# Second attention: GpSimd instead of VectorE makes the low halves of 16 weight tiles

## The chip, the cores and the metric

The kernel runs on one core of a Trainium2 chip. The time is device microseconds (us) of one execution; runs are compared by their median. The engines go by the names of the profile: PE (TensorE, matrix products and transposes), DVE (VectorE), ACT (ScalarE), POOL (GpSimd) and SP (issues most DMAs). PEld is PE's loading of stationary tiles, which runs beside its products.

## The reference, cut to what matters

Two transformer blocks run one after the other on 1024 tokens of width 1024. The change lies in the second. Its attention part is:

```
h = rms_norm_2(x, norm1)
qa, ka, va, fa, qc, kc, vc, gates = split(h @ w_in)
o_a = forgetting_attention(qa, ka, va, log_sigmoid(fa + bias))  # 8 heads, causal
o_b = chunk_band_attention(qc, kc, vc, rel_bias)                # 8 heads, band of 640 keys
g_a, g_b = split(sigmoid(gates))
x = x + (g_a * (o_a @ w_branch_a) + g_b * (o_b @ w_branch_b)) @ w_out
```

All products of weights are float32. The kernel splits a weight tile w and the activations x into a rounded high half and a low half, low = value - high, and adds three products: high by high, high by low and low by high.

## The kernel before, in words

A *unit* is one 128-column tile of a weight matrix, 8 blocks of 128 rows, against all 1024 tokens: 48 matmuls of 128x512. For unit n the tile passes through four hands. SP loads it into `wraw[n % 2]` (`load_w`, L334). ACT copies it rounded into `wh[n % 2]` (`split_hi`, L341), once unit n - 2, which used the buffer before, has been multiplied. Then someone makes `wl[n % 2] = wraw - wh` and raises the semaphore `w_lo`. In all the rest of the program that is POOL (`split_lo`, L346). Last, PE multiplies, and DVE takes the sum out of PSUM.

The second attention (`a2_program_pe`, `_act`, `_dve`, `_sp`; 1826 to 2267 us) runs 8 *pairs* of heads, 4 of the causal kind and then 4 of the band kind, each in 8 steps n of 128 queries. In a step PE makes the scores of step n+2 (L1982, L1985), transposes the probabilities of step n four key blocks at a time (`turn`, L2005; each waits for DVE's scaling and for a free PSUM bank 4), and after each second step multiplies with the values (L2024). Between these PE does `fill`: 1 to 8 matmuls (L1954) of the 16 gate units `U_GATES` to `U_GATES + 15`, so that it has work while the others make the softmax. `FILL` says how many; the units come to an end at 16 fixed places (`UNIT_ENDS`) in the pairs 0 to 6.

DVE does in step n, in this written order: `reciprocal` of the row sums (L2200), two scalings of `pbuf` by them (L2204, `tensor_scalar`, SBUF to SBUF, 128 to 1024 columns wide), the two maxima of step n+2 (L2148, reads PSUM and `bias2`), the low halves of the gate weight tiles whose unit ended a step before (`gate_lo`, L2186), in steps 0 and 5 the low half of an attention output (`low`, L2179), and the copies of the turned probabilities of one head (L2132, PSUM to `pt2`). Where a unit has ended, `gate_evac` (L2168) takes its sum out. That is at the step's end at most places; the next thing on DVE is then the next step's L2200 and L2204, or, at a change of pairs, `begin` and its maxima.

ACT does the copies of the other head (L2134), the exponentials (L2076), and `split_hi` at the end of a step in which a unit ended. `gate_evac(u)` on DVE and `split_hi(u + 2)` on ACT wait for the same event, the last matmul of unit u.

The tile that `gate_lo(u)` or `split_lo` makes there is that of unit u + 2, for u = 0 to 15; the last two are the first tiles of `w_branch`. PE asks for it one whole unit later. SP's load of unit u + 3 waits for `w_lo` of the tile that lay in the same buffer.

Of the kernel before, what the change touches and what calls it, by code (L numbers as in the profile page):

```python
# [8 lines left out]
F32 = mybir.dt.float32  # L9
F32R = mybir.dt.float32r  # L10
ALU = mybir.AluOpType
# [56 lines left out]
U_BRANCH = U_QKV2 + 40  # L68
U_OUT2 = U_BRANCH + KT
U_UP2 = U_OUT2 + KT  # L70
# [39 lines left out]
def build_program(nc, a, out):  # L110
    ctx = ExitStack()
    with ctx:
# [3 lines left out]
        def at(name, offset_kb, shape, dt=F32):  # L116
            return nc.alloc_sbuf_tensor_at(name, shape, dt, offset=base + int(offset_kb * KB))

        def sem(name):
            return ctx.enter_context(nc.semaphore(name))  # L120
# [7 lines left out]
        wh = at("wh", 64, [P, 2, KT, P], F32R)  # L128
        wl = at("wl", 72, [P, 2, KT, P], F32R)
        wraw = at("wraw", 80, [P, 2, KT, P])  # L130
# [56 lines left out]
        def bank2(slot):  # L187
            return ps[:, 2 * slot:2 * slot + 2, :]
# [118 lines left out]
        w_hi = sem("w_hi")  # L307
        w_lo = sem("w_lo")
# [34 lines left out]
        def split_lo(pool, n, s, first=False):  # L343

            pool.wait_ge(w_hi, n + 1)
            nc.gpsimd.tensor_tensor(wl[:, s, :, :], wraw[:, s, :, :], wh[:, s, :, :].bitcast(F32),  # L346
                                    ALU.subtract).then_inc(w_lo, 1)
# [100 lines left out]
        def apart(eng):  # L448


            eng.sem_inc(marks, 1)
# [1344 lines left out]
        def keys_of(b, n):  # L1796
            return range(0 if b < FOX_PAIRS else max(0, n - 4), n + 1)

        def groups_of(b, n):
            return range((len(keys_of(b, n)) + 3) // 4)  # L1800

        def bias_part(b, n):
            size = P * len(keys_of(b, n))
            first = P * (4 - n) if b >= FOX_PAIRS and n < 4 else 0
            return slice(first, first + size)
# [11 lines left out]
        def unit_ends():  # L1817

            ends, made = {}, sum(LEAD)
            for b in range(PAIRS):  # L1820
                made += TURN_FILL[b] + BEGIN[b]
                for n in range(TT):
                    groups = 2 * len(groups_of(b, n))
                    for k in range(groups):
                        count = FILL[b][n][k]
                        for u in range(made // UNIT, (made + count) // UNIT):
                            ends.setdefault((b, n, 2 * k // groups), []).append(u)
                        made += count
            assert made == 16 * UNIT, made
            return ends  # L1830

        UNIT_ENDS = unit_ends()
# [69 lines left out]
        U_GATES = U_QKV2 + QKV2  # L1902
# [218 lines left out]
        def turned_copy(eng, steps, b, n, m, g):  # L2121

            count = min(4, len(keys_of(b, n)) - 4 * g)
            first = keys_of(b, n)[0] + 4 * g
            a2_pe.wait(eng, f"t{b}{n}{m}{g}", 0)
            old = TT // 2 * b + n // 2 - 2
            if old >= 0:
                a2_pe.wait(eng, f"o{old // 4}{old % 4}", 0)
            to = pt2[:, n // 2 % 2, first:first + count, m, n % 2 * P:n % 2 * P + P]
            of = ps[:, TURN_BANK[b, n, m, g], 0:count * P].rearrange("p (k q) -> p k q", k=count)  # L2130
            if m:
                ins = nc.vector.tensor_copy(to, of)  # L2132
            else:
                ins = nc.scalar.activation(to, of, ACT.Copy)  # L2134
            steps.done(ins, f"pt{b}{n}{m}{g}")

        def a2_program_dve(dve):

            def maxima(b, n):
                size = P * len(keys_of(b, n))  # L2140
                a2_pe.wait(dve, f"s{b}{n}", 0)
                step = TT * b + n
                if step >= 3:
                    ob, on = divmod(step - 3, TT)
                    a2_pe.wait(dve, f"t{ob}{on}1{groups_of(ob, on)[-1]}", 0)
                for m in range(2):
                    apart(dve)
                    a2_dve.done(nc.vector.tensor_tensor_reduce(  # L2148
                        pbuf[:, step % 3, m, 0:size], ps[:, 2 * m:2 * m + 2, :].rearrange("p a n -> p (a n)")[:, 0:size],
                        bias2[:, m, bias_part(b, n)], -1.0, 3e38, ALU.add, ALU.min, negmax2[:, n, m:m + 1]),  # L2150
                        f"mx{b}{n}{m}")

            def begin(b):

                dve.wait_ge(a2_bias, 32 * (b + 1) + 96 * max(0, b + 1 - FOX_PAIRS))
                if b >= FOX_PAIRS:
                    for m in range(2):
                        a2_dve.done(nc.vector.memset(bias2[0:64, m, 576:640], NEG), f"e{b}{2 * m}")
                        a2_dve.done(nc.vector.memset(bias2[64:128, m, 0:64], NEG), f"e{b}{2 * m + 1}")
                    a2_dve.wait(dve, f"e{b}3", 0)  # L2160
                maxima(b, 0)

            def gate_evac(u):

                n = U_GATES + u
                dve.wait_ge(mm_done, n + 1)
                dve.wait_ge(stage_stored[0], STAGES1 + 16 * (4 + u))
                nc.vector.tensor_tensor(stage[:, 0, :], bank2(3), rstd[:, :], ALU.mult).then_inc(evac_done, 1)  # L2168

            def low(b, h):  # L2170

                a2_act.wait(dve, f"ot{b}{h}", 0)
                if b < PAIRS - 1:
                    dve.wait_ge(parked_stored[h], 32 * b)
                    lo, hi = ost_lo[:, h, :], ost[:, h, :]
                else:
                    part = slice(h * HALF, (h + 1) * HALF)
                    lo, hi = xl[:, b, part], xh[:, b, part]
                a2_dve.done(nc.vector.tensor_tensor(lo, ps[:, 5, :], hi.bitcast(F32), ALU.subtract), f"xl{b}{h}")  # L2179

            def gate_lo(u):

                n = U_GATES + u + 2
                dve.wait_ge(w_hi, n + 1)
                dve.wait_ge(w_lo, n)
                nc.vector.tensor_tensor(wl[:, n % 2, :, :], wraw[:, n % 2, :, :], wh[:, n % 2, :, :].bitcast(F32),  # L2186
                                        ALU.subtract).then_inc(w_lo, 1)

            for s in range(2):
                dve.wait_ge(hi_stored[s], 16 * 8)  # L2190
                dve.wait_ge(lo_stored[s], 16 * 8)
                dve.wait_ge(stage_stored[s], STAGES1 + 16 * 4)
            lows = []
            begin(0)
            for b in range(PAIRS):
                maxima(b, 1)
                for n in range(TT):
                    size = P * len(keys_of(b, n))
                    a2_act.wait(dve, f"ex{b}{n}1", 0)
                    a2_dve.done(nc.vector.reciprocal(rowsum2[:, n, :], rowsum2[:, n, :]), f"rl{b}{n}")  # L2200
                    a2_dve.wait(dve, f"rl{b}{n}", 0)
                    for m in range(2):
                        part = pbuf[:, (TT * b + n) % 3, m, 0:size]
                        a2_dve.done(nc.vector.tensor_scalar(part, part, rowsum2[:, n, m:m + 1], None, ALU.mult),  # L2204
                                    f"sc{b}{n}{m}")
                    if n + 2 < TT:
                        maxima(b, n + 2)
                    for u in UNIT_ENDS.get((b, n, 0), ()):
                        gate_evac(u)
                    for u in lows:  # L2210
                        gate_lo(u)
                    lows = []
                    if n == 0 and b:
                        low(b - 1, 1)
                    if n == 5:
                        low(b, 0)
                    for g in groups_of(b, n):
                        turned_copy(dve, a2_dve, b, n, 1, g)
                    for u in UNIT_ENDS.get((b, n, 1), ()):
                        gate_evac(u)  # L2220
                    lows += [u for part in range(2) for u in UNIT_ENDS.get((b, n, part), ())]
                    if n == TT - 1 and b + 1 < PAIRS:
                        begin(b + 1)
            low(PAIRS - 1, 1)
# [542 lines left out]
        def _(pool):  # L2767
# [92 lines left out]
            for u in range(QKV2):  # L2860
                split_lo(pool, U_QKV2 + 2 + u, (U_QKV2 + u) % 2)
                if of_qk(u):
                    c = qk_index(u)
                    pool.wait_ge(hl_hi, c + 1)
                    if c >= 2:
                        pool.wait_ge(lo_stored[u % 2], 16 * (c // 2))
                    nc.gpsimd.tensor_tensor(ls[:, u % 2, :], stage[:, u % 2, :], hs[:, u % 2, :].bitcast(F32),
                                            ALU.subtract).then_inc(hl_lo, 1)
            for n in range(U_BRANCH + 2, U_UP2 + 2):
                split_lo(pool, n, n % 2)  # L2870
            with pool.Fori(0, DOWN2 - 1) as c:
                for k in range(2, 4):
# [425 lines left out]
```

## Time and profile before

| | before |
|---|---|
| median of 3 runs | 3165.24 us (3164.25 to 3165.67) |
| the profiled execution: time, span | 3167.0 us, 3165.3 us |
| PE busy | 3027.9 us, 96% of the span |
| DVE busy | 1525.4 us, 48% |
| ACT busy | 968.9 us, 31% |
| POOL busy | 634.3 us, 20%, 276 instructions |
| in 1825 to 2260 us: PE, DVE, ACT, POOL busy | 405.9, 241.1, 175.1, 2.4 us |

Busy time is time in which the engine worked on an instruction; what counts for the kernel's time is which engine the others wait for at a given place. The stretch in the last row is the second attention: PE has work for 406 of its 435 us, and POOL has one instruction in it, the last low half made before the attention began.

### The profile page before, as it was taken

The numbers are of one execution on the slowest core, as the hardware profiler recorded it, in microseconds if no ns is written. First come the engines' busy times: TensorE is split into PE (matmuls) and PEld (weight loads), VectorE is DVE, ScalarE is ACT, GpSimd is POOL, SyncE is SP. The second block draws the span as 40 slices with busy tenths as digits, with TensorE's granted clock in tenths as the row PEclk, the third lists the DMA queues.
The fourth block names the chain that finished last, engine by engine and source line by source line (L and its number), as shares of the span: only waits on it lengthen the run. The fifth ranks groups of instructions, "written<-read, shape, count | busy, mean of one in ns | idle before, by whom it ended". The sixth has DMA issues, their size and how long they took to land.

```text
span 3165.3 us, 48821 instructions
## 1 busy us (share of the span) xinstructions
PE 3027.9 (96%) x20514; PEld 2431.4 (77%) x20514; DVE 1525.4 (48%) x1859; ACT 968.9 (31%) x1438; POOL 634.3 (20%) x276
## 2 busy tenths in 40 slices
PE   8999988888999999999899999999899999999999
PEld 6877867777788888888678867666688888888887
DVE  3166677722644444445711145555553444444445
ACT  3155555623422222222411143334332211111112
POOL 4311122312321222122143300000022222122211
PEclk9999999999999999999899999999999999999999
DMA  6533410022411111111454533444544310111111
GB/s 206 164 99 108 146 70 25 25 76 62 151 47 40 60 46 46 46 40 40 128 168 129 170 113 116 129 143 128 199 138 137 116 49 31 53 53 53 46 33 67
DMA packets 235008, 292.80 MB, mean 93 GB/s; under 512 B 10057, under 2 KB 182226, under 8 KB 234842
## 3 DMA queue, kind: packets, MB, share of 16 engines
q1 hardware_dynamic: 219866, 243.22, 25.1%
q10 hardware_dynamic: 14976, 47.19, 3.9%
q8 instruction: 126, 2.06, 0.3%
q14 instruction: 40, 0.33, 0.0%
HBM read 209.86 MB, written 80.51 MB: 92 GB/s over the span
## 4 chain that ended last, share of the span: by engine, by line
PE 84%; DVE 6%; issue 5%; ACT 2%; DMA 2%; POOL 1%; SPq 0%; DVEq 0%; ACTq 0%; POOLq 0%
PE ps L369 62%; PE ps L1954 4%; PE ps L541 4%; PE ps L1385 4%; PE ps L2005 2%; PE ps L2024 2%; PE ps L1982 1%; PE ps L1448 1%; PE ps L1985 1%; DMA wraw<-in_w_in 1%; DMA residual<-src 1%; DVE cb L2567 1%; DVE y L2463 1%; DVE stage L2168 0%; PE ps L1426 0%
## 5 line engine op out<-in xcount | busy, mean ns | idle before, releaser
L346 POOL TENSOR_TENSOR wl<-wraw,wh 128x1024 fp32r<-128x1024 f32 x151 | 369.1, 2445 | 1672.0 <-ACT wh L341 1672.0
L369 PE MATMUL ps<-xh,wh 128*128 128x512 f32 x2192 | 683.5, 393 | 12.1 <-POOL wl L346 5.2
L369 PE MATMUL ps<-xl,wh 128*128 128x512 f32 x2192 | 678.1, 391 | 0.0
L369 PE MATMUL ps<-xh,wl 128*128 128x512 f32 x2192 | 677.7, 390 | 0.0
L369 PEld LDWEIGHTS ps<-xh,wh 128*128 128x128 f32 x2192 | 410.1, 189 | 110.9 <-issue 12.0
L369 PEld LDWEIGHTS ps<-xl,wh 128*128 128x128 f32 x2192 | 413.4, 189 | 86.8
L369 PEld LDWEIGHTS ps<-xh,wl 128*128 128x128 f32 x2192 | 413.1, 188 | 86.9
L341 ACT ACTIVATE wh<-wraw 128x1024 fp32r<-128x1024 f32 x167 | 177.0, 1060 | 928.2 <-PE ps L369 860.5
L2463 DVE TENSOR_TENSOR y<-ps,y 128x1024 f32<-128x1024 f32 x208 | 253.3, 1222 | 240.3 <-PE ps L369 240.1
L2366 POOL TENSOR_TENSOR dl<-draw,dh 128x2048 fp32r<-128x2048 f32 x25 | 119.1, 4765 | 521.2 <-ACT dh L2362 521.2
L2508 DVE SCALAR_TENSOR_TENSOR cb<-ub,cols,cb 128x1024 f32<-128x1024 f32 x88 | 130.6, 1484 | 61.1 <-ACT cb L2545 56.0
L369 PE MATMUL ps<-dh,fh 128*128 128x512 f32 x480 | 149.4, 392 | 6.0 <-DVE y L2463 6.0
L369 PE MATMUL ps<-dl,fh 128*128 128x512 f32 x480 | 148.0, 389 | 0.0
L369 PE MATMUL ps<-dh,fl 128*128 128x512 f32 x480 | 147.9, 389 | 0.0
L2498 DVE TENSOR_TENSOR ub<-ps,rstd 128x1024 f32<-128x1024 f32 x44 | 53.9, 1225 | 171.9 <-PE ps L369 171.7
L2567 DVE TENSOR_TENSOR cb<-ps,rstd 128x1024 f32<-128x1024 f32 x32 | 39.2, 1225 | 198.0 <-PE ps L369 194.1
L2148 DVE CUSTOM_DVE_ANT_0 pbuf<-ps,bias 128x640 f32<-128x640 f32 (+7 forms) x128 | 85.5, 705 | 97.5 <-PE ps L1990 49.6
L2362 ACT ACTIVATE dh<-draw 128x2048 fp32r<-128x2048 f32 x25 | 47.8, 1913 | 235.3 <-PE ps L369 235.3
L2005 PE MATMUL ps<-ident,pbuf 128*128 128x128 f32 x528 | 93.8, 286 | 20.2 <-DVE pbuf L2204 9.6
L369 PEld LDWEIGHTS ps<-dh,fh 128*128 128x128 f32 x480 | 89.0, 188 | 29.4 <-DVE y L2463 11.5
L2005 PEld LDWEIGHTS ps<-ident,pbuf 128*128 128x128 f32 x528 | 60.9, 143 | 59.3 <-DVE pbuf L2204 17.1
L369 PEld LDWEIGHTS ps<-dl,fh 128*128 128x128 f32 x480 | 90.1, 188 | 19.0
(345 smaller groups left out, 4402.2 us busy)
## 6 DMA issues: line engine op xcount, KB each, us to landing
wraw<-in_w_up SPq DMA_DIRECT2D x76, 512.0 KB, 3.9
wraw<-in_w_in SPq DMA_DIRECT2D x67, 512.0 KB, 4.2
draw<-in_w_down SPq DMA_DIRECT2D x27, 1024.0 KB, 5.0
residual<-src ACTq DMA_DIRECT2D x32, 512.0 KB, 5.0
proj<-stage SPq DMA_DIRECT2D x30, 512.0 KB, 3.0
qk_hi<-hs ACTq DMA_DIRECT2D x24, 512.0 KB, 2.8
qk_lo<-ls SPq DMA_DIRECT2D x24, 512.0 KB, 2.9
kh<-qk_hi SPq DMA_DIRECT2D x48, 256.0 KB, 6.9
```

What stands on the lines that cost most here:

```text
L341: nc.scalar.activation(wh[:, s, :, :], wraw[:, s, :, :], ACT.Copy).then_inc(w_hi, 1)
L346: nc.gpsimd.tensor_tensor(wl[:, s, :, :], wraw[:, s, :, :], wh[:, s, :, :].bitcast(F32), ALU.subtract).then_inc(w_lo, 1)
L369: mm = nc.tensor.matmul(ps[:, bank + h, :], w, x[:, h * HALF:(h + 1) * HALF], start=start and k == 0, stop=stop and k == 2)
L541: return nc.tensor.matmul(to, left, right, **kw)
L1385: ins = mm(ps[:, 2 * fill_slot(u) + h, :], w[:, s, kt, :], x[:, kt, h * HALF:(h + 1) * HALF], start=kt == 0 and part == 0, stop=kt == KT - ...
L1954: ins = mm(ps[:, 6 + h, :], w[:, s, kt, :], x[:, kt, h * HALF:(h + 1) * HALF], start=kt == 0 and part == 0, stop=kt == KT - 1 and part == 2)
L2005: ins = nc.tensor.transpose(ps[:, bank, (k - 4 * g) * P:(k - 4 * g + 1) * P], pbuf[:, (TT * b + n) % 3, m, k * P:(k + 1) * P], ident[:, :])
L2148: a2_dve.done(nc.vector.tensor_tensor_reduce(pbuf[:, step % 3, m, 0:size], ps[:, 2 * m:2 * m + 2, :].rearrange("p a n -> p (a n)")[:, 0:size],
L2366: nc.gpsimd.tensor_tensor(dl[:, :, :], draw[:, :, :], dh[:, :, :].bitcast(F32), ALU.subtract)\
L2463: nc.vector.tensor_tensor(y[:, m, :], bank2(2 + m % 2), y[:, m, :], ALU.add).then_inc(down_added, 1)
L2508: ff1_dve.done(nc.vector.scalar_tensor_tensor(out=cb[:, r, :], in0=ub[:, r, 2 - back:T + 2 - back], scalar=col_at("conv_w", (2 - back) * 2 ...
L2567: nc.vector.tensor_tensor(cb[:, 0, :], bank2((U_UP2 + t) % 2), rstd[:, :], ALU.mult)\
```

## The change

DVE no longer makes any low half. POOL's program gets the 16 calls instead, all in one loop with those that followed. Instructions of PE, ACT and SP, their order and what they wait for stay as they are.

```diff
 # a2_program_dve, gone:
-            def gate_lo(u):
-
-                n = U_GATES + u + 2
-                dve.wait_ge(w_hi, n + 1)
-                dve.wait_ge(w_lo, n)
-                nc.vector.tensor_tensor(wl[:, n % 2, :, :], wraw[:, n % 2, :, :], wh[:, n % 2, :, :].bitcast(F32),
-                                        ALU.subtract).then_inc(w_lo, 1)
...
                         maxima(b, n + 2)
                     for u in UNIT_ENDS.get((b, n, 0), ()):
                         gate_evac(u)
-                    for u in lows:
-                        gate_lo(u)
-                    lows = []
...
-                    lows += [u for part in range(2) for u in UNIT_ENDS.get((b, n, part), ())]
...
 # the program of GpSimd:
-            for n in range(U_BRANCH + 2, U_UP2 + 2):
+            for n in range(U_GATES + 2, U_UP2 + 2):
                 split_lo(pool, n, n % 2)
```

On DVE, at the end of the first gate unit (the unit's sum `stage` is taken out, then the next step's reciprocal, scalings and maxima, then the low half). The lines of the two versions differ by 9; `x2` marks two alike.

```order
 L2132 COPY pt_181<-ps 128x128
 L2168 TENSOR_TENSOR stage<-ps,rstd 128x1024
-L2200 RECIPROCAL rowsum_187<-rowsum_187 128x2
-L2204 TENSOR_SCALAR pbuf<-pbuf,rowsum_187 128x768 x2
+L2191 RECIPROCAL rowsum_187<-rowsum_187 128x2
+L2195 TENSOR_SCALAR pbuf<-pbuf,rowsum_187 128x768 x2
 L2148 ISA pbuf,negmax_186<-ps,bias_182 128x1024
 L2148 ISA negmax_186 128x1
 L2148 ISA pbuf,negmax_186<-ps,bias_182 128x1024
 L2148 ISA negmax_186 128x1
-L2186 TENSOR_TENSOR wl<-wraw,wh 128x1024
 L2179 TENSOR_TENSOR ost_lo<-ps,ost 128x512
```

One row goes, L2186; what stood behind it, `low` (L2179) and the copies, follows the maxima at once. There are 16 such places.

On POOL, around the end of the projections of the second block. Before:

```order
L346 TENSOR_TENSOR wl<-wraw,wh 128x1024 [waits w_hi]
L2867 TENSOR_TENSOR ls<-stage,hs 128x1024 [waits lo_stored1,hl_hi]
L346 TENSOR_TENSOR wl<-wraw,wh 128x1024 [waits w_hi] x20
L2871 UNCONDITIONAL_BRANCH
L2871 ISA
```

And now:

```order
L346 TENSOR_TENSOR wl<-wraw,wh 128x1024 [waits w_hi]
L2854 TENSOR_TENSOR ls<-stage,hs 128x1024 [waits lo_stored1,hl_hi]
L346 TENSOR_TENSOR wl<-wraw,wh 128x1024 [waits w_hi] x36
L2858 UNCONDITIONAL_BRANCH
L2858 ISA
```

The row of 20 low halves (the last 2 projection tiles, the first 2 gate tiles and 16 of later stages) has become one of 36: each of the new 16 waits for `w_hi`, that is for ACT's copy of its own tile, and for nothing else.

## Rows read from the trace of the kernel before

**Rows 1.** The page: the chain that ended last, by engine.

```profile
PE 84%; DVE 6%; issue 5%; ACT 2%; DMA 2%; POOL 1%; SPq 0%; DVEq 0%; ACTq 0%; POOLq 0%
```

**Rows 2.** Groups of the second attention (1825 to 2260 us): busy, mean ns, idle.

```profile
L2186 DVE TENSOR_TENSOR wl<-wraw,wh 128x1024 fp32r<-128x1024 f32 x16 | 19.5, 1221 | 0.0
```

**Rows 3.** Instructions on tile `wl`: ns min/median/max.

```profile
L346 POOL TENSOR_TENSOR wl<-wraw,wh x151: 2342/2402/3369, 14.3 to 3093.8; 128x1024 fp32r<-128x1024 f32 x151
```

**Rows 4.** Timeline of unit end 1857: start, us, engine, line [idle before].

```profile
1857.20 1.06 ACT L341 ACTIVATE wh<-wraw 128x1024 fp32r<-128x1024 f32 x1 [1.20 <-PE ps L1954]
...
1858.47 1.15 DVE L2204 TENSOR_SCALAR pbuf<-pbuf,rowsum 128x768 f32<-128x768 f32 x2
...
1859.14 0.66 PE L2005 MATMUL ps<-ident,pbuf 128*128 128x128 f32 x4
...
1861.82 1.22 DVE L2186 TENSOR_TENSOR wl<-wraw,wh 128x1024 fp32r<-128x1024 f32 x1
...
1864.39 0.41 PE L2005 MATMUL ps<-ident,pbuf 128*128 128x128 f32 x2 [1.10 <-DVE pt L2132]
```

**Rows 5.** Timeline of unit end 2101, a band pair.

```profile
2101.65 1.06 ACT L341 ACTIVATE wh<-wraw 128x1024 fp32r<-128x1024 f32 x1 [0.89 <-PE ps L1954]
...
2102.92 1.02 DVE L2204 TENSOR_SCALAR pbuf<-pbuf,rowsum 128x640 f32<-128x640 f32 x2
...
2103.53 0.66 PE L2005 MATMUL ps<-ident,pbuf 128*128 128x128 f32 x4 [0.85 <-DVE pbuf L2204]
...
2107.91 0.30 PE L2005 MATMUL ps<-ident,pbuf 128*128 128x128 f32 x1 [0.34 <-DVE pt L2132]
```

**Rows 6.** Timeline of unit end 1904, behind step 2 of pair 1.

```profile
1904.84 1.05 ACT L341 ACTIVATE wh<-wraw 128x1024 fp32r<-128x1024 f32 x1
...
1905.99 0.88 DVE L2204 TENSOR_SCALAR pbuf<-pbuf,rowsum 128x512 f32<-128x512 f32 x2
...
1906.53 0.66 PE L2005 MATMUL ps<-ident,pbuf 128*128 128x128 f32 x4 [0.30 <-DVE pbuf L2204]
```

**Rows 7.** PE timeline: first turn behind a `wl` after a pair change.

```profile
2026.76 0.44 PE L2005 MATMUL ps<-ident,pbuf 128*128 128x128 f32 x2 [0.36 <-DVE pbuf L2204]
...
2082.82 0.44 PE L2005 MATMUL ps<-ident,pbuf 128*128 128x128 f32 x2 [0.60 <-DVE pbuf L2204]
...
2134.14 0.44 PE L2005 MATMUL ps<-ident,pbuf 128*128 128x128 f32 x2 [0.96 <-DVE pbuf L2204]
...
2235.33 1.11 PE L2005 MATMUL ps<-ident,pbuf 128*128 128x128 f32 x4 [0.45 <-DVE pbuf L2204]
```

**Rows 8.** Timeline before the attention: ACT `wh`, then GpSimd `wl`.

```profile
1825.62 1.06 ACT L341 ACTIVATE wh<-wraw 128x1024 fp32r<-128x1024 f32 x1 [9.82 <-PE ps L369]
1826.75 2.38 POOL L346 TENSOR_TENSOR wl<-wraw,wh 128x1024 fp32r<-128x1024 f32 x1 [8.48 <-ACT wh L341]
```

**Rows 9.** Timeline of the first block, GpSimd and DVE at once.

```profile
494.66 2.36 POOL L1214 TENSOR_TENSOR rkv<-rkv 128x1024 f32<-128x1024 f32 x1
...
496.33 0.73 DVE L1118 TENSOR_SCALAR y_mean<-y_mean 128x16 f32<-128x16 f32 x1
...
496.97 2.36 POOL L346 TENSOR_TENSOR wl<-wraw,wh 128x1024 fp32r<-128x1024 f32 x1
497.09 3.33 DVE L1120 TENSOR_TENSOR yb<-yb,y_mean 128x1024 f32<-128x1024 f32 x1
```

**Rows 10.** Timeline of the first attention, DVE first by 0.05 us.

```profile
161.08 0.68 DVE L1600 TENSOR_SCALAR abias<-abias 128x1024 f32<-128x1024 f32 x1
161.13 2.89 POOL L346 TENSOR_TENSOR wl<-wraw,wh 128x1024 fp32r<-128x1024 f32 x1 [8.48 <-ACT wh L341]
```

**Rows 11.** PE timeline: the first matmuls behind two stalls.

```profile
576.95 1.97 PE L541 MATMUL ps<-mm_um,mm_n 64*64 64x64 f32 x118 [1.63 <-issue]
...
696.91 1.22 PE L369 MATMUL ps<-xh,wh 128*128 128x512 f32 x2 [2.11 <-POOL xl L1222]
```

**Rows 12.** Stretch behind the second stall: us, busy (x), PEclk, DMA, GB/s.

```profile
697.00:700.20 3.20, 3.20 (x8) 2.55 (x9) 0.00 (x0) 0.27 (x1) 0.00 (x0) 0.50 0.00 0
```

More of the change, by code:

```diff
@@ L2209, in a2_program_dve @@
                         gate_evac(u)
-                    for u in lows:
-                        gate_lo(u)
-                    lows = []
                     if n == 0 and b:
```

## Prediction

> **What bounds the kernel now.** I read the page first. The chain that ended last is 84% PE and 6% DVE [rows 1], so what counts here is where PE waits for DVE in the second attention. The groups of that stretch give what is moved: 16 instructions of 1.22 us, with no idle time before any [rows 2], so DVE never waits for the rounded tile. The view by tile gives the price on POOL: median 2.40 us, twice as much, and a longest of 3.37 [rows 3]. Then the timeline at each of the 16 unit ends; it shows four kinds.
>
> Kind 1, four places, behind step 4 of pairs 0 to 3 [rows 4]. The unit's last matmul releases ACT (`wh`, 1857.20 to 1858.26) and DVE (`stage`) together. DVE then scales from 1858.47; PE takes up its turn at 1859.14, as soon as the first scaling is done, and later waits 1.10 us (to 1864.39) for a copy that stands behind `wl` and `low` in DVE's row. Kind 2, three places, behind step 4 of pairs 4 to 6 [rows 5]: PE waits 0.85 us for the scaling and later 0.34 for the copy. Kind 3, two places, behind step 2 of pairs 1 and 2 [rows 6]: PE waits 0.30 us for the scaling; none of its waits comes from `wl`. Kind 4, seven places, at a change of pairs: the next step begins with maxima, a scaling comes only behind the next scores, and `wl` comes later, in step 0. PE's turn behind it waits 0.36, 0.60, 0.96, 0.60 (as in the second row) and 0.45 us in five of them [rows 7]; in pairs 1 and 2 the longer fills cover it.
>
> **What the change takes away.** 1.13 us of DVE's row at each place (next start less own start). PE can gain no more than its idle time: 4 x 1.10 + 3 x 0.34 in kinds 1 and 2, and 0.36 + 2 x 0.60 + 0.96 + 0.45 = 2.97 us in kind 4. All together 4.40 + 1.02 + 2.97 = 8.4 us, if nothing else moved.
>
> **What it adds.** POOL's own time is hidden: it is idle here, a low half takes 2.40 us, and PE wants that tile only a whole unit later, some 23 us on (unit 0 ends at 1857, unit 2 at 1904) [rows 4, 6]. SP's load of unit u + 3 waits for the low half of unit u + 1, which is older still; ACT's order is the same. Were that cover gone, PE would wait up to 2.4 us a unit.
>
> The new thing is when POOL works: just when DVE wants to scale. Where the two overlap, the trace shows them in turns, not side by side. A `tensor_scalar` that began 1.67 us into a POOL instruction ended at 497.06, 0.04 behind POOL's end at 497.02, though it is only 16 columns wide. A `tensor_tensor` with both inputs in SBUF that began 0.12 us behind POOL's `wl` took 3.33 us and ended 1.09 us behind it, that is its usual 1.22 less 0.13 [rows 9]. The other way round, DVE 0.05 us ahead with a fast `tensor_scalar` (0.68 us for 1024 columns) stretched POOL's `wl` to 2.89 us, 0.49 more [rows 10]. L2204 is that same fast kind: two times 768 columns in 1.15 us [rows 4]. The maxima, `stage` and the copies read PSUM and one SBUF input at most; I cost them at nothing, and if they too were held, kinds 1 and 2 would be no worse (they queue behind the scaling) and kind 4 would lose up to 2 us each.
>
> Who comes first: POOL starts its `wl` 0.07 us behind the end of ACT's `wh` [rows 8]. In kind 1 that is 1858.33, against DVE's scaling at 1858.47: POOL leads by 0.13 us. In kind 2 it is 2102.78 against 2102.92, the same [rows 5]. A lead of 0.12 was enough in rows 9. In kind 3 it is 1905.96 against 1905.99, a lead of 0.03 [rows 6] (about 0.06 at the other); no row decides so close a race, since the closest with DVE ahead is 0.05 [rows 10]. So kind 3 costs between nothing (DVE goes first) and the full delay (POOL goes first). I take the full delay, since POOL's recorded start is the earlier in both.
>
> The Trainium skill (SBUF — State Buffer, Who interferes with whom) says that the pair of ports that DVE and GpSimd share is an exclusive lock, for DVE in its two-port modes and for DVE with two SBUF inputs, and that "Issue order, not op shape, decides who blocks". By that rule this change puts GpSimd first at nine places; with kind 3 held the sum below is 11.1 us, and without it 6.6. The trace agrees with the rule at 0.12 us; the close race is not in it.
>
> Delay of a scaling: kind 1, POOL ends at 1858.33 + 2.40 = 1860.73; the first scaling (0.6 us alone) ends about 0.5 later, at 1861.23 instead of 1859.09: 2.14 us. PE's next work up to its wait is 1859.14 to 1863.29 (1864.39 less 1.10), which now ends at 1865.43; DVE's copy is due at 1864.39 + 2.14 - 1.13 = 1865.40. The later one counts. PE goes on at 1865.43 instead of 1864.39, **1.04 us late, times 4 = 4.2**. Kind 2: the same 2.14 us. PE's work ends at 2107.57 + 2.14 = 2109.71 instead of going on at 2107.91: **1.80 us, times 3 = 5.4**. Kind 3: POOL ends at 1908.36, the scaling (half of 0.88, and a little) at 1908.72 instead of 1906.48: **2.24 us, times 2 = 4.5**; PE has no idle time behind it that could give any back. Kind 4 gains **3.0**. Sum: 4.2 + 5.4 + 4.5 - 3.0 = **11.1 us slower**.
>
> **The clock.** PE now stands still for 2.2 us (kind 1), 3.0 (0.85 + 2.14, kind 2) and 2.5 (0.30 + 2.24, kind 3). In this trace a stall of 1.63 us was followed by full speed, 118 small products at once; behind one of 2.11 us the first two 128x512 matmuls took 1.22 us, and the granted clock was 0.50 for the next 3.2 us (1.2 instead of 2.4 GHz) [rows 11, 12]. While the clock is halved PE, which has no cover behind such a stall, does half its work: some 1.5 us lost each time, at most 1.6. All nine new stalls are longer than 2.11 us. Nothing shows that each one is followed by a drop; between 0 and 9 is possible, so 0 to 14 us. I take 6: the three of kind 2, one or two of kind 3, one or two of kind 1. That is 9 us.
>
> **Sum.** 11.1 + 9 = 20 us. The profiled execution took 3167.0 us, 1.7 more than its span, and 1.8 above the median of the runs; it would become 3187, and the median 3165.2 + 20 = 3185.
>
> **The rivals.**
> 1. *The same, but the clock stays up* (nought to two drops): 11 to 14 us slower, 3177 to 3179. For it: the stalls are short, and the rows have only a few of that length. Chance 0.18.
> 2. *DVE wins the close races of kind 3*: 6.6 us, with about 5 drops 14, so 3172 to 3180. Against it: POOL's start is first. Chance 0.20.
> 3. *No turns at all between L2204 and POOL's `wl`*: then only the gains are left, 3165.2 - 8.4 = 3157. The deciding point is whether the wide scaling, alone among the fast `tensor_scalar`, runs beside POOL. It speaks against it that a 16-column one and a 1024-column one both did not [rows 9, 10]. Or DVE starts its scaling first: it would need a `wh` that ends 0.13 us later. Chance 0.06.
> 4. *It nets out*: POOL leads at fewer places than I read, or the delay is hidden by fills, so that the gains of 8.4 stand against losses of about that size. Chance 0.06.
>
> My own forecast has 0.50. The range reaches from rival 2 with few drops up to all nine drops (11.1 + 14 = 25) and a little: 3170 to 3192.5. A measurement of this kernel tells apart about 0.2%, here 6.3 us; faster by more than that is rival 3, 0.06; within it rival 4 and the low end of rival 2, 0.08; slower the rest, 0.86.
>
> **What the profile after would show.** In kinds 1 and 2 the first L2204 of the step takes about 2.8 us instead of 0.6 and ends about 0.5 us behind POOL's `wl`; PE's turn behind it has 2.2 and 3.0 us of idle time before it, ended by DVE `pbuf`. PE's 1.10 and 0.34 us waits for the copy are gone or near nothing. In kind 3 either DVE or POOL is stretched, and which one settles the race. In kind 4 PE's five waits are gone and `wl` of POOL is 2.4 us long. The granted clock shows new stretches at 0.50 right behind the stalls. The forecast fails if L2204 keeps its 0.6 us while POOL runs, or if the clock falls behind none of the stalls, or stays down for several times 3.2 us.

## The result, and the profile after

| | before | after |
|---|---|---|
| median | 3165.37 us (3164.25 to 3168.26, 5 runs) | 3187.32 us (3179.74 to 3190.66, 5 runs) |
| the profiled execution: time, span | 3167.0, 3165.3 us | 3190.7, 3188.6 us |

The ratio is 1.006 (1.0043 to 1.0076), and the medians are 22 us apart (0.7%, within that interval): the kernel is slower. The five executions after took 3179.7, 3179.8, 3187.3, 3189.3 and 3190.7 us, at mean granted clocks of 0.989, 0.988, 0.985, 0.984 and 0.985; the profile is that of the slowest. One of the 12 executions of a later run, e3, took 5018 us at a mean granted clock of 0.555; what caused it is not known, and it is left out of e3's median.

The page of the kernel after, busy times, chain and the group of POOL's low halves (busy, mean ns, idle before):

```profile
PE 3037.9 (95%) x20514; PEld 2440.3 (77%) x20514; DVE 1526.1 (48%) x1843; ACT 968.6 (30%) x1438; POOL 671.7 (21%) x292
...
PE 85%; DVE 5%; issue 5%; ACT 2%; DMA 2%; POOL 1%; SPq 0%; DVEq 0%; ACTq 0%; POOLq 0%
...
L346 POOL TENSOR_TENSOR wl<-wraw,wh 128x1024 fp32r<-128x1024 f32 x167 | 406.6, 2435 | 1654.4 <-ACT wh L341 1654.4
```

At this distance little is to be seen: the chain reads nearly as before [rows 1], and POOL has 16 instructions more, at 21% of the span. PE is busy 10.0 us longer, though it executes the same instructions. The windows over the attention say more. First before, then after (us, then busy time and count of PE, PEld, DVE, ACT and POOL, granted clock, DMA share, GB/s):

```profile
1825.00:2260.00 435.00, 405.92 (x2376) 286.58 (x2375) 241.06 (x601) 175.13 (x397) 2.38 (x1) 0.98 0.44 137
```

```profile
1828.00:2284.00 456.00, 415.65 (x2379) 295.48 (x2378) 242.35 (x585) 175.19 (x398) 40.10 (x17) 0.96 0.43 131
```

The stretch is 21 us longer. PE's busy time rose by 9.7 us and its idle time (the width less the busy time) from 29.1 to 40.3, by 11.3. DVE's did not fall, though 19.5 us of low halves are gone from it. So there are two losses of about the same size, PE standing still and PE working slower. The groups of L2005, PE's turns, name the first; here are the rows of before and of after, over these two stretches:

```profile
L2005 PE MATMUL ps<-ident,pbuf 128*128 128x128 f32 x509 | 91.1, 287 | 18.6 <-DVE pbuf L2204 8.4 <-DVE pt L2132 7.1 <-ACT pt L2134 2.3
```

```profile
L2005 PE MATMUL ps<-ident,pbuf 128*128 128x128 f32 x514 | 95.0, 295 | 28.4 <-DVE pbuf L2195 24.1 <-ACT pt L2134 2.3 <-DVE pt L2132 1.6
```

The idle time that DVE's copy ended (`pt`) went from 7.1 to 1.6 us: this is the gain. What the scaling ended (`pbuf`) went from 8.4 to 24.1: this is the price. The lines moved up by 9: L2204 of before is L2195 now.

In all timelines a row gives the start in us, the time it took in us, engine, line, what it wrote and read, how many instructions it merges, and in brackets the idle time before it and what ended it.

Where it happens is seen in the timeline. Kind 1, to be read against [rows 4]:

```profile
1859.86 1.06 ACT L341 ACTIVATE wh<-wraw 128x1024 fp32r<-128x1024 f32 x1 [1.21 <-PE ps L1954]
...
1861.00 2.35 POOL L346 TENSOR_TENSOR wl<-wraw,wh 128x1024 fp32r<-128x1024 f32 x1 [29.18 <-ACT wh L341]
...
1861.14 3.16 DVE L2195 TENSOR_SCALAR pbuf<-pbuf,rowsum 128x768 f32<-128x768 f32 x2
...
1863.82 0.78 PE L2005 MATMUL ps<-ident,pbuf 128*128 128x128 f32 x4 [2.11 <-DVE pbuf L2195]
...
1869.44 0.41 PE L2005 MATMUL ps<-ident,pbuf 128*128 128x128 f32 x2
```

POOL starts 0.14 us ahead of DVE's two scalings. They take 3.16 us instead of 1.15, the first one 2.63; it ends at 1863.77, 0.42 behind POOL's 1863.35. PE stands still for 2.11 us. The wait for the copy, 1.10 us before, is gone from the last row. Kind 2, against [rows 5], and kind 3, against [rows 6]:

```profile
2119.22 2.34 POOL L346 TENSOR_TENSOR wl<-wraw,wh 128x1024 fp32r<-128x1024 f32 x1 [28.60 <-ACT wh L341]
...
2119.35 3.02 DVE L2195 TENSOR_SCALAR pbuf<-pbuf,rowsum 128x640 f32<-128x640 f32 x2
...
2121.96 0.66 PE L2005 MATMUL ps<-ident,pbuf 128*128 128x128 f32 x4 [2.85 <-DVE pbuf L2195]
...
2125.94 0.30 PE L2005 MATMUL ps<-ident,pbuf 128*128 128x128 f32 x1
```

```profile
1911.01 2.34 POOL L346 TENSOR_TENSOR wl<-wraw,wh 128x1024 fp32r<-128x1024 f32 x1 [22.04 <-ACT wh L341]
1911.05 2.98 DVE L2195 TENSOR_SCALAR pbuf<-pbuf,rowsum 128x512 f32<-128x512 f32 x2
...
1913.69 0.66 PE L2005 MATMUL ps<-ident,pbuf 128*128 128x128 f32 x4 [2.40 <-DVE pbuf L2195]
```

The same picture with stalls of 2.85 and 2.40 us. In kind 3 POOL leads by 0.04 us and goes first. Behind the changes of pairs the turns that waited for the scaling before [rows 7] start without a wait now.

The second loss is the clock. First come two pairs of windows from kind 1, each a stall and then the work behind it; the last row is the work behind the last stall of kind 2 (columns as above; the clock is the number after POOL's):

```profile
1861.70:1863.80 2.10, 0.01 (x1) 0.00 (x0) 2.10 (x2) 0.00 (x0) 1.65 (x1) 1.00 0.93 318
1864.30:1867.50 3.20, 3.20 (x11) 2.51 (x10) 2.88 (x5) 1.33 (x3) 0.00 (x0) 0.50 0.99 230
2006.20:2008.30 2.10, 0.01 (x1) 0.00 (x0) 2.10 (x2) 0.00 (x0) 1.65 (x1) 1.00 0.91 310
2008.40:2011.60 3.20, 3.20 (x20) 2.59 (x20) 3.20 (x6) 2.00 (x4) 0.00 (x0) 1.00 1.03 257
2227.30:2232.70 5.40, 5.40 (x18) 4.42 (x19) 2.40 (x6) 2.49 (x6) 0.00 (x0) 0.50 1.05 242
```

Behind the stall that ended at 1863.8 the granted clock was 0.50, which is 1.2 instead of 2.4 GHz. Behind an equal stall that ended at 2008.3 it stayed at 1.00. Behind the one that ended at 2227.2 it was 0.50 for all of the 5.4 us.

From one start of ACT's `wh` to the next, every unit can be compared with before. This table is worked out from those starts, in the two profiled executions:

| kind | places compared | us more, no clock fall | us more, with one |
|---|---|---|---|
| 1 | 4 | 0.89 | 2.38, 2.43, 2.42 |
| 2 | 3 | 1.60 | 3.13, 4.09 |
| 3 | 2 | 2.08 | 4.83 |
| 4 | 6 | 0.00, -0.03, -0.56, -0.68, -1.07, -0.66 | none |

Together +20.8 us between the `wh` that starts ahead of the attention (1825.6 before, 1828.3 after) and the last one (398.6 before, 419.5 after). The rest of the 23.3 us between the two spans, 2.5, lies outside this stretch: that first `wh` comes 2.7 us later than before, and up to it both kernels execute the same instructions.

Not every fall of the clock in the attention belongs to the change. In the last pair of heads, where PE has no fills left, the kernel before has one too, of over 13 us:

```profile
2230.63 0.61 PE L1982 MATMUL ps<-kh,qs 128*128 128x384 f32 x2 [1.06 <-DVE negmax L2148]
...
2232.93 1.22 PE L1982 MATMUL ps<-kh,qs 128*128 128x512 f32 x2 [0.95 <-DVE negmax L2148]
```

```profile
2226.00:2232.90 6.90, 4.92 (x38) 3.00 (x37) 2.95 (x17) 3.79 (x12) 0.00 (x0) 1.00 0.96 341
2232.90:2246.50 13.60, 11.97 (x44) 7.88 (x45) 8.97 (x25) 4.88 (x15) 0.00 (x0) 0.50 1.03 408
```

There no wait of PE was longer than 1.06 us. This pair lies behind the last `wh`, so it is in the windows over the attention but not in the table.

### The profile page after: what moved, and what is told of

Its sections match the earlier page's. It is cut to its first block, busy times and chain, and to the rows that moved or that the text cites. A ratio compares the mean times of both kernels' runs of the same rounds, so it can differ in the third digit from the quotient of the medians.

```text
span 3188.6 us, 48805 instructions
## 1 busy us (share of the span) xinstructions
PE 3037.9 (95%) x20514; PEld 2440.3 (77%) x20514; DVE 1526.1 (48%) x1843; ACT 968.6 (30%) x1438; POOL 671.7 (21%) x292
## 4 chain that ended last, share of the span: by engine, by line
PE 85%; DVE 5%; issue 5%; ACT 2%; DMA 2%; POOL 1%; SPq 0%; DVEq 0%; ACTq 0%; POOLq 0%
PE ps L369 61%; PE ps L1954 5%; PE ps L541 4%; PE ps L1385 4%; PE ps L2005 2%; PE ps L2024 2%; PE ps L1982 1%; DVE pbuf L2195 1%; PE ps L1448 1%; PE ps L1985 1%; DMA wraw<-in_w_in 1%; DVE cb L2554 1%; DVE y L2450 0%; DMA residual<-src 0%; DVE stage L2168 0%
## 5 line engine op out<-in xcount | busy, mean ns | idle before, releaser
L346 POOL TENSOR_TENSOR wl<-wraw,wh 128x1024 fp32r<-128x1024 f32 x167 | 406.6, 2435 | 1654.4 <-ACT wh L341 1654.4
L2005 PE MATMUL ps<-ident,pbuf 128*128 128x128 f32 x528 | 97.1, 294 | 30.0 <-DVE pbuf L2195 25.3
L2005 PEld LDWEIGHTS ps<-ident,pbuf 128*128 128x128 f32 x528 | 63.5, 147 | 68.7 <-DVE pbuf L2195 32.0
L369 PEld LDWEIGHTS ps<-dh,fl 128*128 128x128 f32 x480 | 90.1, 188 | 19.0
```

Source lines behind the costliest of these rows:

```text
L369: mm = nc.tensor.matmul(ps[:, bank + h, :], w, x[:, h * HALF:(h + 1) * HALF], start=start and k == 0, stop=stop and k == 2)
L2005: ins = nc.tensor.transpose(ps[:, bank, (k - 4 * g) * P:(k - 4 * g + 1) * P], pbuf[:, (TT * b + n) % 3, m, k * P:(k + 1) * P], ident[:, :])
```

## The experiments

All times are medians; each ratio is against the kernel before in runs on the same chip, where its median was 3165.4 us (after), 3165.8 (e1 to e4) and 3165.0 (e5 to e7). The last column is read from the profiled execution of each run.

| run | us | ratio (95%) | first `wh` to last, against before |
|---|---|---|---|
| after | 3187.32 | 1.0060 (1.0043 to 1.0076) | +20.8 |
| e1_after_scaling | 3154.40 | 0.9962 (0.9949 to 0.9975) | -8.7 |
| e2_pair_ends | 3161.64 | 0.9983 (0.9974 to 0.9992) | -2.6 |
| e3_third_kind | 3172.80 | 1.0024 (1.0013 to 1.0034) | +5.5 |
| e4_sliver | 3154.46 | 0.9963 (0.9949 to 0.9976) | -8.6 |
| e5_fill_first | 3177.52 | 1.0036 (1.0022 to 1.0049) | +15.8 |
| e6_pool_late | 3184.58 | 1.0060 (1.0046 to 1.0074) | +17.7 |
| e7_pool_later | 3170.67 | 1.0017 (1.0008 to 1.0026) | +6.1 |

**e1_after_scaling: the same low halves on POOL, but behind the scalings.** At the nine places of kinds 1 to 3 POOL first waits for the event of the next step's second scaling.

```diff
-            for n in range(U_GATES + 2, U_UP2 + 2):
+            ends = {u: (b, n) for (b, n, part), us in UNIT_ENDS.items() for u in us}
+            for u in range(16):
+                b, n = ends[u]
+                if n + 1 < TT:
+                    a2_dve.wait(pool, f"sc{b}{n + 1}1", 0)
+                split_lo(pool, U_GATES + u + 2, (U_GATES + u) % 2)
+            for n in range(U_BRANCH + 2, U_UP2 + 2):
```

> GpSimd still makes all 16 low halves, but at the nine places of kinds 1 to 3 it waits for the second scaling of the next step. Theory (the loss is the scaling held behind GpSimd, and the clock that falls behind the stalls): the gains alone are left, 4 x 1.10 + 3 x 0.34 + 3.0 = 8.4 us, so 3157 us, no stall over 1 us before a turn behind a unit end, and no stretch at half clock there. Rival (GpSimd at work also holds the maxima, `low` or the copies on DVE, or its slowness reaches PE): each of the nine places costs up to 2 us, so 3165 us or more.

Timeline of a place of kind 1:

```profile
1859.64 1.15 DVE L2195 TENSOR_SCALAR pbuf<-pbuf,rowsum 128x768 f32<-128x768 f32 x2
...
1860.32 0.66 PE L2005 MATMUL ps<-ident,pbuf 128*128 128x128 f32 x4
1860.71 1.22 DVE L2148 CUSTOM_DVE_ANT_0 pbuf<-ps,bias 128x1024 f32<-128x1024 f32 x1
...
1860.88 2.41 POOL L346 TENSOR_TENSOR wl<-wraw,wh 128x1024 fp32r<-128x1024 f32 x1 [30.58 <-DVE pbuf L2195]
...
1864.43 0.41 PE L2005 MATMUL ps<-ident,pbuf 128*128 128x128 f32 x2
```

The two scalings have their 1.15 us back, PE's first turn has no wait, and neither has the last row, where PE waited 1.10 us in the kernel before. POOL's 2.41 us now lie beside the maxima (1.22 us here) and, in kinds 1 and 2, the start of `low` (0.69 us). These took as long as without POOL beside them, and POOL within 0.04 us of its 2.38 at the changes of pairs. The copies come only behind POOL's end here, so this run does not test them. It is 11.4 us faster than before: its ratio is 0.9962, where that of the kernel after is 1.0060. The profiled execution was the slowest of the six (3163.4 us); what the change gained is seen between the `wh`, 8.7 us, and the other 2.7 are not traced to it. The one wait decides it: what costs time is not that POOL does the work, but that it does it while DVE scales.

**e4_sliver: POOL's instruction at the same moment, but tiny.** POOL subtracts 1 of 128 columns of each block. The rest of the low halves of these 16 tiles is left out of the computation.

```diff
+                if n < U_BRANCH + 2:
+                    pool.wait_ge(w_hi, n + 1)
+                    nc.gpsimd.tensor_tensor(wl[:, n % 2, :, 0:1], wraw[:, n % 2, :, 0:1],
+                                            wh[:, n % 2, :, 0:1].bitcast(F32), ALU.subtract).then_inc(w_lo, 1)
+                    continue
```

> As the changed kernel, at the same places, but in the attention GpSimd subtracts only 1 of 128 columns of each of the 8 blocks (8 elements a partition instead of 1024); the rest of those 16 low halves is left out. Theory (the length of GpSimd's hold counts): the scaling is held for about 0.2 us at most, so nearly the whole gain of 8.4 us: 3157 to 3159 us. Rival (the handover to GpSimd or DVE's new order costs): near the changed kernel, 3175 us or more.

```profile
1856.89 0.22 POOL L2859 TENSOR_TENSOR wl<-wraw,wh 128x8 fp32r<-128x8 f32 x1 [29.19 <-ACT wh L341]
...
1857.03 1.15 DVE L2195 TENSOR_SCALAR pbuf<-pbuf,rowsum 128x768 f32<-128x768 f32 x2
```

Both rows are from the timeline of kind 1. POOL still starts 0.14 us ahead, but it is done after 0.22 us, and the scalings keep their 1.15. The time agrees with e1's within their intervals. So e1 left no part of the price behind: POOL's low half beside the maxima and `low` costs as little as an instruction of 0.22 us. And the loss of the kernel after goes with the length of POOL's instruction, not with the event that starts it.

**e2_pair_ends and e3_third_kind: one kind alone.** DVE keeps its low halves except at the changes of pairs (e2), or except at the two places of kind 3 (e3).

```diff
...
+        def on_pool(u):
+            b, n = END_OF[u]
+            return n == TT - 1        # e3: return n == 2
...
+            for u in range(16):
+                if on_pool(u):
+                    pool.wait_ge(w_lo, U_GATES + u + 2)
+                    split_lo(pool, U_GATES + u + 2, (U_GATES + u) % 2)
```

> GpSimd makes only the seven low halves whose unit ends at a change of pairs; DVE makes the other nine as before. Theory: no scaling is near, so only the gain of kind 4 is left, 3.0 us: 3162.4 us. Rival (any GpSimd work in the attention costs time): 3165 us or more.

> GpSimd makes only the two low halves behind step 2 of pairs 1 and 2, where its lead over the scaling is 0.03 to 0.06 us; DVE makes the other 14 as before. Theory: GpSimd wins both races, 2 x 2.1 us, and the clock falls behind one or both stalls, 1.5 to 5 us more: 3171 to 3175 us. Rival (a race so close can go to DVE in other executions): 3165 us in some or all rounds, with GpSimd's instruction stretched instead.

e2 is faster than before by 4.2 us, of which 2.6 are found between the `wh`: kind 4 is a gain that stands alone. e3 is 7.0 us slower. Its two places cost 3.72 (with a clock fall) and 2.14 us. The timeline of the first one:

```profile
1905.06 3.04 DVE L2211 TENSOR_SCALAR pbuf<-pbuf,rowsum 128x512 f32<-128x512 f32 x2
1905.08 2.34 POOL L346 TENSOR_TENSOR wl<-wraw,wh 128x1024 fp32r<-128x1024 f32 x1 [76.93 <-ACT wh L341]
...
1907.76 1.12 PE L2010 MATMUL ps<-ident,pbuf 128*128 128x128 f32 x4 [2.46 <-DVE pbuf L2211]
```

DVE's recorded start is 0.02 us ahead of POOL's (0.01 at the second place), and yet it is the scaling that is stretched and POOL that keeps its 2.34 us. The recorded start is not the moment that decides.

**e5_fill_first: something for PE to do during the stall.** At the nine places the first fill of the step stands ahead of its first turn. The low halves are made as in the kernel after.

```diff
+                    ahead = any((b, n - 1, part) in UNIT_ENDS for part in range(2))
...
+                            if ahead and k == 0:
+                                fill(FILL[b][n][k])
+                                turn(b, n, m, g)
+                            else:
+                                turn(b, n, m, g)
+                                fill(FILL[b][n][k])
```

> As the changed kernel, but in the nine steps behind kinds 1 to 3 PE does the first fill (4 matmuls, 8 in kind 3) before the first turn instead of behind it. The scaling is held as long as before, yet PE's stall is cut: 1.2 us instead of 2.1 in kind 1, 1.9 instead of 2.85 in kind 2, 0.55 instead of 2.4 in kind 3. The second turn still waits for ACT's copy out of the bank, so kinds 1 and 2 give nothing back by themselves, kind 3 some 0.9 us each. Theory (behind the shorter stalls the clock stays up): 4 x 0.9 + 3 x 1.6 + 2 x 1.2 - 3.0 = 7.8 us over before, 3173 to 3176 us. Rival (the lock alone makes the loss, the clock has no part): 3185 us.

Timelines of a place of kind 1 and of one of kind 2. The windows are those of two places of kind 1, the first from behind both stalls and the second from behind the first stall on, and then of two places of kind 2, from behind the first stall on; the last row repeats the first 1.8 us of the third, up to the end of its second stall:

```profile
1858.28 0.66 PE L2005 MATMUL ps<-ident,pbuf 128*128 128x128 f32 x4 [1.16 <-DVE pbuf L2200]
...
1859.71 0.41 PE L2005 MATMUL ps<-ident,pbuf 128*128 128x128 f32 x2 [0.78 <-ACT pt L2139]
```

```profile
2104.70 2.37 POOL L346 TENSOR_TENSOR wl<-wraw,wh 128x1024 fp32r<-128x1024 f32 x1 [28.59 <-ACT wh L341]
...
2107.47 1.11 PE L2005 MATMUL ps<-ident,pbuf 128*128 128x128 f32 x4 [1.43 <-DVE pbuf L2200]
...
2109.36 0.45 PE L2005 MATMUL ps<-ident,pbuf 128*128 128x128 f32 x1 [0.78 <-DVE negmax L2153]
```

```profile
1859.70:1863.00 3.30, 3.29 (x18) 2.58 (x19) 2.71 (x7) 2.65 (x5) 0.00 (x0) 1.00 1.04 236
1926.90:1930.20 3.30, 2.52 (x16) 2.06 (x17) 3.30 (x7) 2.10 (x5) 0.00 (x0) 1.00 1.01 238
2107.50:2114.10 6.60, 5.82 (x19) 4.46 (x20) 3.16 (x7) 2.49 (x6) 0.00 (x0) 0.50 1.05 242
2162.00:2168.70 6.70, 5.92 (x19) 4.56 (x20) 3.12 (x7) 2.49 (x6) 0.00 (x0) 0.50 1.04 238
2107.50:2109.30 1.80, 1.09 (x4) 0.68 (x4) 1.80 (x6) 0.60 (x1) 0.00 (x0) 0.50 1.10 280
```

In kinds 1 and 3 the stalls of 2.11 and 2.40 us became two, of 1.16 and 0.78 and of 0.55 and 0.78, and the clock stayed up. These places cost 0.9 each, as the undisturbed one of kind 1 did, and 1.3 (kind 3, from 2.08). In kind 2 the stalls are 1.43 and 0.78, with 1.1 us of turns between them, and at all three places the clock was at 0.50 for the whole window: 4.2 us each, more than in the kernel after. It was down before the second stall came: the four products between the two took 1.11 us instead of 0.66. That is why the time is 1.5 us above what was expected. What the run does show: with a fill in the gap the clock stayed up at all six places of kinds 1 and 3, where it had fallen at four in the kernel after, and the loss without the clock is left nearly whole in kind 1, since DVE is just as late.

**e6_pool_late and e7_pool_later: who is first.** Ahead of its low half POOL fills columns of a table that is no longer needed (`tri`): twice 4 columns in e6, six times 1 column in e7.

```diff
...
+                if n < U_BRANCH + 2:
+                    pool.wait_ge(w_hi, n + 1)
+                    for k in range(6):                 # e6: range(2), 4 columns each
+                        c = 8 * (n - U_GATES - 2) + k
+                        nc.gpsimd.memset(tri[:, c:c + 1], 0.0).then_inc(late, 1)
```

> As the changed kernel, but GpSimd fills two times 4 columns of a scratch tile ahead of each of the 16 low halves, so that it comes about 0.2 us later and DVE's first scaling is some 0.07 us ahead of it. Theory (whoever starts first goes first): the first scaling is in time, PE's first turn has no stall over 1 us. If GpSimd goes next, the second scaling is held and the sum is 3160 to 3168 us; if the second scaling goes next too, 3154 to 3157 us. Rival (DVE is held whenever GpSimd has work, the order does not matter): near 3185 us.

> As the last, with six one-column fills ahead of each low half, about 0.6 us: GpSimd's low half comes due while the second scaling runs. Theory: both scalings go first, GpSimd behind them, 3154 to 3158 us, as with the wait for the scaling. Rival (GpSimd holds the shared ports with its small fills too, or gets in between): 3160 us or more, with a scaling stretched.

e6 failed as an experiment on kinds 1 and 2: its two fills of 0.10 us overlapped and moved POOL by only about 0.07 us, so that POOL was still first there, by 0.06, and the ratio is that of the kernel after. In kind 3 it brought the order that the trace of before could not decide:

```profile
1905.78 0.14 POOL L2862 MEMSET tri<- 128x4 f32 x2 [21.96 <-ACT wh L341]
1905.84 3.05 DVE L2195 TENSOR_SCALAR pbuf<-pbuf,rowsum 128x512 f32<-128x512 f32 x2
1905.87 2.34 POOL L346 TENSOR_TENSOR wl<-wraw,wh 128x1024 fp32r<-128x1024 f32 x1
...
1908.54 0.66 PE L2005 MATMUL ps<-ident,pbuf 128*128 128x128 f32 x4 [2.46 <-DVE pbuf L2195]
```

POOL's recorded start is 0.03 us behind DVE's (0.04 at the other place), and POOL still wins. In the kernel before a DVE 0.05 ahead had won [rows 10]. In e7 the six fills took 0.27 us and moved POOL by 0.22, to 0.07 behind DVE (0.16 in kind 3):

```profile
1858.79 0.27 POOL L2862 MEMSET tri<- 128x1 f32 x6 [29.17 <-ACT wh L341]
...
1858.94 3.28 DVE L2195 TENSOR_SCALAR pbuf<-pbuf,rowsum 128x768 f32<-128x768 f32 x2
1859.01 2.80 POOL L346 TENSOR_TENSOR wl<-wraw,wh 128x1024 fp32r<-128x1024 f32 x1
...
1859.62 0.66 PE L2005 MATMUL ps<-ident,pbuf 128*128 128x128 f32 x4
...
1865.85 0.41 PE L2005 MATMUL ps<-ident,pbuf 128*128 128x128 f32 x2 [1.99 <-DVE pt L2132]
```

Now the first scaling is done in its usual time, 0.62 us, PE's turn at 1859.62 has no wait, and it is POOL that is stretched, to 2.80 us. But DVE's two scalings still end only at 1862.22, 0.41 behind POOL's end: between them POOL came in. The second one, and all that is queued behind it on DVE, is as late as in the kernel after, and PE pays 1.99 us at the copy, where it had paid 1.10 before. I had expected that DVE, once first, stays first, and a time below the kernel before; it was 5.7 us above, and the rival named with that expectation, that POOL gets in between, is what happened. To be ahead is not enough, POOL has to be kept out until the last scaling is done, as e1 does.

## Why the prediction was right, and where its sizes were off

The forecast was 3185, +20 us; measured were 3187.3, +22. Against the terms of its sum, as the two profiled executions have them:

| term | predicted | measured |
|---|---|---|
| kind 1, each of 4 | +1.04 | +0.89 |
| kind 2, each of 3 | +1.80 | +1.60 |
| kind 3, each of 2 | +2.24 | +2.08 |
| kind 4 | -3.0 | -2.97 in four places; a fifth not settled |
| sum without the clock | +11.1 | +9.5 |
| clock falls | 6 times 1.5 = 9 | 6, together 11.3 |

- *Two instructions in turns*: right, at all nine places. The price per place was 0.15 to 0.20 us too high, by about the same in each kind, most of it from one quantity, the delay of the first scaling. I had 2.14 us; it is 2.02 (2.63 instead of about 0.6). POOL took 2.35 and not 2.40, and the scaling ended 0.42 behind it and not 0.5. The rule of the Trainium skill (SBUF — State Buffer, Who interferes with whom) that the issue order decides who blocks was borne out at a lead of 0.14 us for POOL, and in the other direction by e7, with DVE 0.07 ahead.
- *The close races of kind 3*: right in the outcome, the full delay. The reason given, POOL's recorded start being earlier, was weaker than it looked: in e3 and e6 it was the later one at all four places, by 0.01 to 0.04 us, and POOL won as well.
- *Kind 4*: the waits of 0.36, 0.60, 0.96 and 0.60 us gave back 0.56, 0.68, 1.07 and 0.66. In each place it is 0.06 to 0.20 more than the wait; from what is not settled. The fifth place lies behind the last `wh`, where executions differ by more than its 0.45.
- *The clock*: the count was right in the profiled execution, but its spread over the kinds was not: three in kind 1, two in kind 2, one in kind 3, where I had put all three of kind 2. The premise was right, that a stall of over 2 us is often but not always followed by a fall. The 6 itself was a choice between 0 and 9, and that it was hit is luck: e6, with nine stalls of 2.2 to 2.9 us, has five falls. The bound was wrong: "some 1.5 us lost each time, at most 1.6". Four falls cost 1.49 to 1.54. The other two lasted longer, and cost 2.75 (4.83 less 2.08) and 2.49 (4.09 less 1.60). The bound came from one window of 3.2 us [rows 12]; the same trace had the fall of over 13 us shown above. The prediction named a clock that stays down for longer as what would break it; with two it moved the sum by 2.3 us.
- *The executions differ*: two of the five took 3179.7 and 3179.8 us, at a higher mean clock than the profiled one. That is within 1 us of the 3177 to 3179 of rival 1, in which the clock hardly falls. Only the profiled execution shows its falls one by one, so how many the other four had is open; the six are those of the slowest.
- *What the change takes away*: the bound of 8.4 us was nearly right. Without the wait behind the last `wh` (0.45) it is 7.95 for the stretch between the `wh`, where e1, which pays no price, won 8.7: 0.01 to 0.05 us more than the wait at each place of kinds 1 and 2, and in kind 4 as above.
- The errors had opposite signs, -1.6 and +2.3, so that the sum came closer than its terms is luck too.

Not tried: a scaling of the same width in a slower form, which would tell whether only the fast form is held up, and DVE's copies beside POOL. Which of two equal stalls is followed by a clock fall stays open as well.

## What to carry to other kernels

Work that moves to GpSimd has a price where it overlaps an SBUF-to-SBUF instruction of VectorE that someone waits for: look at who starts first, to a tenth of a microsecond, and count nearly the whole of GpSimd's instruction as the price (2.0 us of 2.35 here). Beside VectorE's maxima, which read PSUM, it cost nothing here. Where the result isn't due for long, one wait on the last of those VectorE instructions turns the loss into the gain: here from +22 us to -11. A new stall of TensorE should be costed as a range, with and without work behind it at half the clock. Here there is no safe length: stalls of 2.1 to 2.9 us were followed by a fall at six of nine places (the profile after), one of 1.99 at one of four (e7), one of 1.43 at three of three (e5), and 1.16 with 0.78 at none of four (e5).

## What the runs showed of the hardware that was not expected

- Who is first is decided close to, but not at, the recorded starts: POOL won at 0.14 to 0.04 us ahead and at 0.01 to 0.04 behind; DVE won when it was 0.05 [rows 10], 0.07 and 0.16 ahead (e7). The Trainium skill (Perfetto Trace Analysis, GPSIMD Engine Instruction) says that a GpSimd instruction's reported start is the moment one of its processors issues its first tensor read. Nothing here shows when the port is asked for.
- Two scalings that follow each other on DVE without a gap do not keep POOL out: it came in between them at all nine places of e7.
- A stall of 1.43 us was followed by 6.6 us and more at clock 0.50 all three times (e5), though one of 1.63 had not been [rows 11], and in the kernel before the clock fell with no wait above 1.06 us in the 8 us ahead of it. So the length of the last stall alone does not tell.
- Six small fills on POOL took 0.27 us together, though each is recorded with 0.10: they start 0.03 us apart. The low half behind them started 0.22 us after the first.
